# Dot products ahead of remainders, coefficients ahead of roundings, weighing three slabs behind, and GpSimd makes a quarter of the remainders

## The reference

```python
def peer_ffn(h, w_pq, subkeys, u, v):        # 8 heads x 16 picks = 128 rows of u and v for each token
    ...
    expert_idx = jnp.take_along_axis(cand_i, fin_pos, axis=-1)
    gates = jax.nn.softmax(fin_s, axis=-1).astype(h.dtype)
    ...
        u_sel = jnp.take(u, ec, axis=0)
        act = jax.nn.gelu(jnp.einsum('chkd,cd->chk', u_sel, hc), approximate=False) * gc
        v_sel = jnp.take(v, ec, axis=0)
        return jnp.einsum('chk,chkd->cd', act, v_sel)
...
def swiglu(u, w_gate, w_up, w_down):
    return (jax.nn.silu(u @ w_gate) * (u @ w_up)) @ w_down
...
    for l in range(DEPTH):
        h = h + 0.5 * swiglu(rmsnorm(h, ffn1_norm[l]), ffn1_w_gate[l], ffn1_w_up[l], ffn1_w_down[l])
        h = h + hybrid_mixer(rmsnorm(h, mix_norm[l]), pos, k_top, w_in[l], w_ret_out[l], w_att_out[l], w_mix_out[l])
        h = h + 0.5 * swiglu(rmsnorm(h, ffn2_norm[l]), ffn2_w_gate[l], ffn2_w_up[l], ffn2_w_down[l])
```

## Time and profile before

| | us |
|---|---|
| median of 3 runs | 3621.05 |
| fastest and slowest of them | 3619.95, 3626.57 |
| the profiled execution's own time | 3624.96 |
| its span | 3623.2 |

### The profile page before, as it was taken

How to read it: one execution, slowest core, us unless ns; L and a number is a source line. 1 busy time by engine, 2 the same in 40 slices (tenths; PEclk the granted TensorE clock), 3 DMA queues, 4 the chain that set the end, 5 groups by cost and what they waited for, 6 DMA issues and landing times.

```text
span 3623.2 us, 50298 instructions
## 1 busy us (share of the span) xinstructions
PE 3195.1 (88%) x18818; PEld 2506.2 (69%) x18818; DVE 2557.0 (71%) x4577; ACT 1520.6 (42%) x3103; POOL 798.5 (22%) x577
## 2 busy tenths in 40 slices
PE   7998889978887777798899979778999999999998
PEld 6886679844342111677777667656799988998898
DVE  6997243777776877787677777877867576768665
ACT  3222234244443333444344444544545444444443
POOL 1001246133445655222122223222200000000000
PEclk9999999989999999899799999989999999999999
DMA  3322224579999999799788889778956844453454
GB/s 125 96 93 76 70 93 138 179 297 412 412 417 412 412 403 410 290 392 365 287 340 324 319 332 416 287 279 333 387 171 189 266 137 139 126 183 111 135 186 157
DMA packets 185565, 923.56 MB, mean 255 GB/s; under 512 B 21777, under 2 KB 27153, under 8 KB 119521
## 3 DMA queue, kind: packets, MB, share of 16 engines
q0 software_dynamic: 73728, 536.90, 36.9%
q1 hardware_dynamic: 99248, 358.66, 29.6%
q10 hardware_dynamic: 12352, 24.87, 2.2%
HBM read 910.98 MB, written 9.37 MB: 254 GB/s over the span
## 4 chain that ended last, share of the span: by engine, by line
PE 60%; DMA 13%; DVE 13%; ACT 6%; issue 5%; POOL 3%; ACTq 0%; DVEq 0%; POOLq 0%
PE psum L735 47%; DMA buffer_float<-in_peer_uv,buffer_uint 7%; PE psum L1093 7%; DMA raw_slabs<-in_slabs 5%; DVE buffer_float L2646 3%; ACT slabs_rounded L1479 2%; POOL buffer_float L3326 2%; DVE slabs_remainder L2339 1%; PE psum L1316 1%; DVE buffer_float32r L2245 1%; DVE norm_recip_root L2253 1%; ACT buffer_float L1805 1%; PE psum L1301 1%; ACT buffer_float L1798 1%; DVE buffer_float L2802 1%
## 5 line engine op out<-in xcount | busy, mean ns | idle before, releaser
L735 PE MATMUL psum<-buffer_float32r,slabs_rounded 128*128 128x256 f32 (+2 forms) x9568 | 1958.5, 304 | 67.8 <-POOL slabs_remainder L3311 30.1
L735 PEld LDWEIGHTS psum<-buffer_float32r,slabs_rounded 128*128 128x128 f32 x9568 | 1549.9, 193 | 235.6 <-issue 133.1
L735 PE MATMUL psum<-buffer_float32r,slabs_remainder 128*128 128x256 f32 (+2 forms) x4784 | 1442.0, 301 | 0.0
L2339 DVE TENSOR_TENSOR slabs_remainder<-raw_slabs,slabs_rounded 128x1024 fp32r<-128x1024 f32 x601 | 733.0, 1223 | 484.9 <-ACT slabs_rounded L1479 475.5
L1479 ACT ACTIVATE slabs_rounded<-raw_slabs 128x1024 fp32r<-128x1024 f32 x662 | 695.4, 1055 | 751.8 <-PE psum L735 597.2
L3326 POOL DMA_INDIRECT buffer_float<-in_peer_uv,buffer_uint x512 | 651.0, 1272 | 1321.2 <-PE psum L1093 610.0
L735 PEld LDWEIGHTS psum<-buffer_float32r,slabs_remainder 128*128 128x128 f32 x4784 | 921.6, 193 | 29.5
L1093 PE MATMUL psum<-buffer_float,buffer_float 128*64 128x512 f32 x1728 | 634.8, 647 | 268.7 <-ACT buffer_float L1805 254.7
L2646 DVE CUSTOM_DVE_ANT_0 buffer_float<-buffer_float,buffer_float 128x1024 f32<-128x1024 f32 x512 | 622.9, 1221 | 152.0 <-DMA buffer_float<-in_peer_uv,buffer_uint 149.7
L1093 PEld LDWEIGHTS psum<-buffer_float,buffer_float 128*64 128x64 f32 x1728 | 164.6, 143 | 632.1 <-issue 610.5
L1793 ACT ACTIVATE buffer_float<-buffer_float 128x1 f32<-128x1 f32 x512 | 100.1, 195 | 372.3 <-DVE buffer_float L2646 369.4
(11 more groups left out here) (214 smaller groups left out, 2083.3 us busy)
## 6 DMA issues: line engine op xcount, KB each, us to landing
raw_slabs<-in_slabs SPq DMA_DIRECT2D x682, 512.0 KB, 4.0
buffer_float<-in_peer_uv,buffer_uint POOLq DMA_INDIRECT x512, 11.6
buffer_float<-kept ACTq DMA_DIRECT2D x4, 874.5 KB, 6.0
buffer_float<-rows ACTq DMA_DIRECT2D x12, 256.0 KB, 10.1
xT<-in_xT ACTq DMA_DIRECT2D x4, 512.0 KB, 5.5
buffer_float<-in_consts ACTq DMA_DIRECT2D x8, 256.0 KB, 3.7
kept<-buffer_float ACTq DMA_DIRECT2D x4, 512.0 KB, 6.2
buffer_float<-kept ACTq DMA_DIRECT2D x2, 875.0 KB, 7.3
```

The lines of the kernel that those rows point to most:

```text
L735: m = pe.matmul(out, a, b, start=start and j == 0, stop=stop and j == 2)
L2339: dve.tensor_tensor(slab_l[:, r, :], raw[:, r, :], slab_h[:, j, :].bitcast(F32), ALU.subtract)\
```

## The change

Four things change in the woven half. The sums that are computed stay the same.

1. ScalarE makes the coefficients of its place t ahead of rounding slab t+3, not behind it.
2. VectorE does the dot products of place t ahead of the remainder of slab t+3, not behind it.
3. TensorE weighs up to `woven_by(t - 3)` in place of `woven_by(t - 2)`. TURN becomes [63, 118, 171, 230]. VectorE's adds keep `woven_by(t - 2)`.
4. Of the slabs 163 to 420 those whose number divides by four, 65 in all, get their remainder from GpSimd in place of VectorE; 57 of them while picks are left, 31 in the mixer. GpSimd's stream now interleaves them: for each slab t it issues the gathers up to seven beyond what `added_by(t - 1)` counts, then the remainder of slab t+3 where it is one of them, which waits for that slab's rounding.

```diff
--- before.py
+++ after.py
@@ -210,7 +210,7 @@
 
 def turn_after(n):
 
-    return next(t for t in range(BLOCK2) if woven_by(t - 2) >= n)
+    return next(t for t in range(BLOCK2) if woven_by(t - 3) >= n)
 
 
 BOUNDS = [GROUP * (j + 1) for j in range(WOVEN // GROUP)]
@@ -226,7 +226,7 @@
     return n
 
 
-def added_by(t, behind=2):
+def added_by(t, behind=3):
 
     return held(woven_by(t - behind), t)
 
@@ -234,6 +234,11 @@
 def rows_by(t):
 
     return held(woven_by(t - 2), t)
+
+
+def by_pool(q):
+
+    return BLOCK1 + 3 <= q < BLOCK1 + BLOCK2 and q % 4 == 0
 
 
 def by_dve(n):
@@ -1856,10 +1861,11 @@
                 nonlocal turned
                 t = place[0]
                 place[0] += 1
+                if t < BLOCK2:
+                    coefficients(woven_by(t - 1))
                 if BLOCK1 + t + 3 < SLABS:
                     split_ahead()
                 if t < BLOCK2:
-                    coefficients(woven_by(t - 1))
                     if t in TURN:
                         turned = acc.take()
                         if t < TURN[-1]:
@@ -2821,12 +2827,13 @@
 
                 t = place[0]
                 place[0] += 1
-                if BLOCK1 + t + 3 < SLABS:
-                    slab_remainder(BLOCK1 + t + 3)
                 if t < BLOCK2:
                     while woven[0] < woven_by(t):
                         dot(PURE + woven[0])
                         woven[0] += 1
+                if BLOCK1 + t + 3 < SLABS and not by_pool(BLOCK1 + t + 3):
+                    slab_remainder(BLOCK1 + t + 3)
+                if t < BLOCK2:
                     while added[0] < rows_by(t):
                         if by_dve(PURE + added[0]):
                             add_row(PURE + added[0])
@@ -3304,16 +3311,17 @@
                 for n in range(a, b):
                     one_remainder(n)
 
-            def one_remainder(n):
+            def one_remainder(n, n_rounded=None):
 
                 j, r = n % READY, n % LOW
-                pool.wait_ge(slab_rounded, n + 1)
+                pool.wait_ge(slab_rounded, n_rounded or n + 1)
                 pool.tensor_tensor(slab_l[:, r, :], raw[:, r, :], slab_h[:, j, :].bitcast(F32), ALU.subtract)\
                     .then_inc(slab_ready[j], 1)
 
             remainders(0, READY)
             remainders(SPLIT_BY_DVE, WHOLE[0])
-            for n in range(QT * PICKS):
+            def gather(n):
+
                 tt, p = divmod(n, PICKS)
                 slot, turn = n % SLOTS, n // SLOTS
                 if n == 0:
@@ -3326,6 +3334,17 @@
                 pool.indirect_dma_start(uv_rows[slot], None, peer_uv_d,
                                         bass.IndirectOffsetOnAxis(eidx[n // GROUP][:, n % GROUP:n % GROUP + 1], 0))\
                     .then_inc(uv_landed[slot], 16)
+
+            issued = PURE
+            for n in range(issued):
+                gather(n)
+            for t in range(BLOCK2):
+                while issued < min(PURE + SLOTS + added_by(t - 1), QT * PICKS):
+                    gather(issued)
+                    issued += 1
+                if by_pool(BLOCK1 + t + 3):
+                    one_remainder(BLOCK1 + t + 3, rounded_with(BLOCK1 + t + 3))
+            assert issued == QT * PICKS
 
         assert totals[0] == totals[1] == totals[2], totals
 
```

## The result

The changed kernel takes 3593.65 us, the median of four runs (3591.35 to 3596.61), beside 3620.50 before (four runs). The ratio is 0.9926, with a 95% interval of 0.9907 to 0.9945: some 27 us faster. The forecast was 3564 with a range of 3515 to 3625. The time lies in the range, and the sign is right, but of the 57 us of the sum less than half came. The profiled execution has a span of 3594.8 us, 28.4 less than the 3623.2 of before. In all that follows a kernel's time is given as its ratio to runs of the kernel before on the same chip; one thousandth is 3.6 us.

What follows compares the result with a forecast made beforehand. TensorE, busy 3195 of 3623 us, was taken to bound the kernel, with 95.7 us of waits on ScalarE's diagonal. Terms -7-13-5-49+12+5+0 = -57 gave 3564 us; own range 3530 to 3590, whole range 3515 to 3625.

Steps and rivals of the forecast that it cites:

- rival 1: Woven half: late gathers hold dot products, so TensorE still waits on the same diagonal; 3596 us, chance 0.20.
- the mixer's term: Mixer: 49 us gained, from waits on the diagonal and 9 us of faster TensorE clock.
- -7, -13 and -5: First up and gate, down part and second up and gate: us gained there, in that order.
- the rest, 36.8, should go nearly whole: Mixer: of 57.9 us of waits on the diagonal, 36.8 lie outside the excepted ones; 35 taken as gain.
- the 12 and 5 us set against it: Slots freed a slab later: 12 us lost to bunched gathers at three group ends, 5 to later gathers.
- The 7.7 us: Gathers' reserve: dot product 17.0 us after issue, landing in 9.3; slots 4.1 us later leave 3.6, costing nothing there.
- GpSimd's remainders, 0: Woven half: moving 57 remainders from VectorE to GpSimd while picks run neither gains nor costs time, 0 us.
- rival 4: Remainders on GpSimd hold VectorE up to 2.4 us each, freeing 1.2: 68 us lost, 3632 us, chance 0.07.
- all three lengthen the time between a dot product and the weighing: Coefficients ahead takes out a 1.06 us rounding, dots ahead a 1.22 us remainder, later weighing gives 4.1 us.
- Rival 2: Gathers wait behind GpSimd's remainders; the mixer's 31 remainders add 74 us; 3687 us, chance 0.13.
- those for right: Diagonal waits below 40 us, down part about 110, mixer clock above 0.92, `kept` wait 12.74 stays, no TensorE wait names GpSimd.
- those for wrong: Dot products wait over 50 us for gathers; gathers behind GpSimd's remainders; TensorE waits for remainders; saturated stretch outgrows other gains.

Runs made afterwards that it cites:

- e6: The kernel before with TensorE three slabs behind and the group ends one slab later, nothing else: ratio 0.9858 to before.
- e9: The kernel before with VectorE's dot products ahead of the remainder, nothing else: ratio 0.9873 to before.
- e2: The changed kernel with TensorE weighing two slabs behind again: ratio 0.9835 to before.
- e7: The kernel before with GpSimd's 65 remainders, nothing else: ratio 1.0008 to before.
- e8: The kernel before with the two reorderings alone, coefficients ahead of roundings and dot products ahead of remainders: ratio 0.9829 to before.
- e1: The changed kernel with all remainders of the woven half back on VectorE: ratio 0.9853 to before.
- e10: The kernel before with dot products ahead of remainders and TensorE three slabs behind, nothing else: ratio 0.9827 to before.
- e13: The changed kernel where GpSimd only waits for the rounding at its 65 places and VectorE makes all remainders: ratio 0.9894 to before.
- e5: The kernel before with ScalarE's coefficients ahead of the rounding, nothing else: ratio 1.0219 to before.
- e4: The changed kernel with ScalarE's coefficients behind the rounding again: ratio 0.9879 to before.

## Why the prediction was half right

The sum had 57 us, and 27 came. The time lies in the range because the range was wide enough for rival 1 too; the forecast's own range, 3530 to 3590, missed it. The step that failed is the mixer's term, with the two that were set against it. The step behind it is that the reserve of the gathers was charged with one edit at a time, and the reorderings with nothing.

**What bounds the kernel.** Right for the swiglu parts: -7.9, -17.7 and -4.8 measured, for -7, -13 and -5. The wait on the diagonal was the right row there. It fell from 95.7 to 25.3 us. Of the means, it was the third slab that freed the down part: it took 103.0 us with that edit alone (e6), 105.1 with all four, and 111.1 with the dot products ahead alone (e9).

**The mixer, -49.** Wrong, +1.4 together with the two terms of what comes back. The failed step is "the rest, 36.8, should go nearly whole", together with the 12 and 5 us set against it. The waits did go, 57.9 to 21.8 us in the mixer, but others took their place: TensorE's idle time there is 98.0 us, where it was 97.0, and VectorE waits 89.0 us for gathers, where it waited 2.2. Nor did the 9 us of clock come. The mixer in one row of the stretches, with the columns of the earlier trace rows, before, of the changed kernel, and of e2:

```profile
1777.00:2491.00 714.00, 617.10 (x3642) 477.84 (x3643) 528.47 (x839) 323.98 (x705) 173.22 (x149) 0.92 0.84 323
```

```profile
1749.00:2464.00 715.00, 617.00 (x3641) 478.84 (x3641) 530.73 (x806) 323.22 (x705) 265.20 (x179) 0.92 0.85 325
```

```profile
1755.00:2428.00 673.00, 603.37 (x3641) 468.29 (x3641) 535.83 (x806) 325.24 (x705) 262.31 (x180) 0.94 0.89 343
```

The granted clock (the number behind POOL's) is 0.92 before and in the changed kernel, and TensorE is busy for the same 617 us; in e2 the clock is 0.94, the busy time 603 and the idle time 69.7. The waits of more than 3 us show the same: 61 us of them in the mixer before, 60 in the changed kernel, 45 in e2. It could have been had: e2, with all but the third slab, makes the mixer 673.2, that is -40.6.

**Slots freed a slab later, "which costs nothing there".** The 7.7 us were a fair reading (the median over the first up and gate is 9.1), but each edit was held against them alone, and the dot products ahead not at all. The traces show what is left from a gather's landing to its dot product, as the median over the mixer's 150 picks: 10.9 us before, 8.9 with GpSimd's remainders alone (e7), 6.4 with the two reorderings (e8), 5.6 with the third slab alone (e6), 3.1 with the reorderings and the third slab (e1), and 1.8 in the changed kernel, where 56 dot products started within 0.2 us of the landing (6 before). Slower DMAs are not the reason: in the mixer a gather lands in 10.1 us (median), 9.5 before, while the time from its issue to its dot product fell from 19.1 to 13.2. So the reorderings, counted as slack, took 4.5 us of the same reserve. GpSimd's wait came on top (1.9 us more on the average gather, 17.63 in the place shown). A thin reserve is not yet a loss: e10 has 2.8 us and is among the fastest. e1 and e2 show that GpSimd's remainders or the third slab can be borne without the other (26 and 33 us back when one goes), e6 and e7 that neither costs alone. Taken together, the mixer's three terms were 33 us off.

**GpSimd's remainders, 0.** That VectorE gains nothing is right, and shown by e7 (1.0008). VectorE's operations beside a GpSimd remainder were 68 us longer in the changed kernel, against 57 x 1.22 = 70 us taken off it. The bound of the sum (rival 4, 68 us lost) took 2.4 us of hold for each; it was 1.2 on average, and so the account is even. But the remainders cost 26 us in this kernel, 15 by the wait and 12 by the subtraction (e13). Rival 4's condition, dot products that come late, was there all the same. The forecast looked at TensorE's and VectorE's side of them, and took the wait for the rounding as "a slab or so" only in the saturated stretch.

**The two reorderings.** The step "all three lengthen the time between a dot product and the weighing" took them for slack that costs nothing. Coefficients ahead alone make the kernel 79 us slower (e5), and dot products ahead alone 46 us faster without touching the wait on the diagonal (e9). I had read the two streams each by itself; what counts is the loop across both. Beside the third slab the coefficients ahead gave nothing (e10 against e1), and in the changed kernel they cost 17 us (e4).

**Rivals.** Rival 1 gave 3596, 2 us from the time, by the mechanism that came: late gathers and dot products that wait. It had 0.20. That the number agrees so well is in part luck: it let the mixer gain 24 us less 12 at the group ends and the two up and gate parts nothing, where the mixer gained nothing and those parts 12.7. Rival 2's mechanism, GpSimd in front of gathers, is there too, with 323.4 us of waits, but cost 15 us (e13), not 74. They were not two cases but one.

**The signs.** Of those for right, two came: the diagonal at 25.3 us and the down part at 105. The mixer's clock stayed at 0.92, ScalarE's wait for `kept`, which was to stay at 12.74 us, is 2.6 us, and TensorE waits 2.7 us for remainders of GpSimd. Of those for wrong, dot products waited 118.6 us for gathers, gathers stood behind GpSimd's remainders, and TensorE waited 5.6 us for remainders of either engine. The saturated stretch grew by 9 us, less than the others shrank.

**Not forecast.** The part behind the last pick grew by 5.3 us. Eight of GpSimd's remainders stand there, where there is no gather left and nothing to relieve. In the changed kernel a remainder of GpSimd and an operation of the norm on VectorE that TensorE waits for start together:

```profile
2664.47 2.37 POOL L3318 TENSOR_TENSOR slabs_remainder<-raw_slabs,slabs_rounded 128x1024 fp32r<-128x1024 f32 x1 [7.52 <-ACT slabs_rounded L1484]
...
2664.51 2.63 DVE norm_recip_root L2259
```

With no remainder of GpSimd beside it the same norm operation takes 0.44 us there. All kernels with GpSimd's remainders have 101.5 to 103.2 us in this part, and those without 97.9 to 99.6.

## What to carry to other kernels

Moving work ahead in one in-order stream moves a wait ahead as well: follow the loop through every engine that takes part (rounding, remainder, dot product, coefficient here) before counting a reordering as slack. Edits that each take a part of the same reserve must be summed against it, and a wait of an engine that feeds the DMAs counts against that reserve even where the engine is idle for most of the time. And a test of each part alone and of each part taken back is worth more than the sum: the kernel got faster when any one of three of the four edits was left out, while two of them, each by itself, gave nearly twice what all four did.
